# A new order of chunks and post-work in the up-projection, with the reads back of the transposed blocks issued by ScalarE

## The reference

```python
def conv_ffn(h, w_up, conv_w, conv_b, w_down):
    u = causal_dwconv(h @ w_up, conv_w, conv_b)      # D_FF = 5632, width-3 depthwise conv over tokens
    gate, val = jnp.split(u, 2, axis=-1)
    return (jax.nn.gelu(gate) * val) @ w_down

x = x + conv_ffn(rmsnorm(x, norm_ffn[l]), ffn_w_up[l], ffn_conv_w[l], ffn_conv_b[l], ffn_w_down[l])
```

## Time and profile before

| | |
|---|---|
| median of 3 runs | 2179.55 us (2175.43 to 2180.16) |
| the profiled execution | 2177.84 us |
| its span in the profile | 2176.1 us |
| PE busy | 2167.0 us |
| DVE busy | 1706.7 us |
| ACT busy | 1360.0 us |
| granted TensorE clock | 1.0 over the whole span |

### The profile page before, as it was taken

The page is one execution under the profiler, slowest core; times in us unless marked ns, Lnnn a source line. Parts: engine busy times, 40 slices in busy tenths (PEclk is TensorE's granted clock), DMA queues, the critical chain, the costliest instruction groups (busy, mean ns, idle before and its releaser), DMA issues.

```text
span 2176.1 us, 28498 instructions
## 1 busy us (share of the span) xinstructions
PE 2167.0 (100%) x9780; PEld 1795.9 (83%) x9780; DVE 1706.7 (78%) x1968; ACT 1360.0 (63%) x1950; POOL 16.6 (1%) x48
## 2 busy tenths in 40 slices
PE   9999999999999999999999999999999999999999
PEld 8888888887888888888888888888888888888887
DVE  7877866788888887887776676577888888878875
ACT  6654445677777777655555555556777777766553
POOL 2000000000000000000000000000000000000000
PEclk9999999999999999999999999999999999999999
DMA  8666667777777787666676777567877787777774
GB/s 276 218 210 211 200 191 242 218 236 239 246 248 239 245 253 237 208 223 213 228 245 201 233 263 242 186 220 217 257 229 253 229 255 232 257 237 217 238 246 156
DMA packets 269357, 500.15 MB, mean 230 GB/s; under 512 B 18928, under 2 KB 56832, under 8 KB 269136
## 3 DMA queue, kind: packets, MB, share of 16 engines
q1 hardware_dynamic: 267408, 492.78, 71.3%
q0 software_dynamic: 1424, 5.60, 0.7%
q10 hardware_dynamic: 432, 0.56, 0.1%
HBM read 457.15 MB, written 41.71 MB: 229 GB/s over the span
## 4 chain that ended last, share of the span: by engine, by line
PE 82%; DVE 7%; DMA 4%; ACT 3%; issue 3%; SPq 0%; ACTq 0%; DVEq 0%
PE ps L1186 16%; PE ps L1188 16%; PE ps L1187 16%; PE ps L1081 7%; PE ps L1083 7%; PE ps L1082 7%; PE ps L1058 4%; DMA h<-turn_line 2%; PE ps L1092 2%; PE ps L1094 2%; PE ps L1093 2%; DVE w_lo L1419 2%; PE ps L1062 2%; ACT w_hi L620 1%; DMA raw<-w_down 1%
## 5 line engine op out<-in xcount | busy, mean ns | idle before, releaser
L1419 DVE TENSOR_TENSOR w_lo<-raw,w_hi 128x1024 fp32r<-128x1024 f32 x744 | 897.9, 1222 | 347.2 <-ACT w_hi L620 334.6
L620 ACT ACTIVATE w_hi<-raw 128x1024 fp32r<-128x1024 f32 x744 | 770.9, 1053 | 441.4 <-PE ps L1188 165.2
L1186 PE MATMUL ps<-w_hi,xs 128*128 128x512 f32 x1904 | 743.2, 390 | 0.3 <-DVE w_lo L1419 0.3
L1187 PE MATMUL ps<-w_lo,xs 128*128 128x512 f32 x1904 | 740.8, 389 | 0.0
L1188 PE MATMUL ps<-w_hi,xs 128*128 128x512 f32 x1904 | 740.8, 389 | 0.0
L1186 PEld LDWEIGHTS ps<-w_hi,xs 128*128 128x128 f32 x1904 | 357.4, 188 | 75.7 <-DVE w_lo L1419 2.1
L1188 PEld LDWEIGHTS ps<-w_hi,xs 128*128 128x128 f32 x1904 | 357.4, 188 | 74.6
L1187 PEld LDWEIGHTS ps<-w_lo,xs 128*128 128x128 f32 x1904 | 357.5, 188 | 73.5
L1081 PE MATMUL ps<-w_hi,act 128*128 128x512 f32 x736 | 286.9, 390 | 0.4 <-DVE w_lo L1419 0.2
L1082 PE MATMUL ps<-w_lo,act 128*128 128x512 f32 x736 | 286.4, 389 | 0.0
L1083 PE MATMUL ps<-w_hi,act 128*128 128x512 f32 x736 | 286.4, 389 | 0.0
(11 more groups left out here) (312 smaller groups left out, 2004.8 us busy)
## 6 DMA issues: line engine op xcount, KB each, us to landing
raw<-w_up SPq DMA_DIRECT2D x352, 512.0 KB, 4.4
raw<-w_in SPq DMA_DIRECT2D x191, 512.0 KB, 4.5
raw<-w_down SPq DMA_DIRECT2D x176, 512.0 KB, 4.8
turn_line<-cross SPq DMA_DIRECT2D x284, 128.0 KB, 2.4
h<-turn_line SPq DMA_DIRECT2D x71, 512.0 KB, 5.3
raw<-w_out SPq DMA_DIRECT2D x64, 512.0 KB, 4.8
prob_line<-probs_t SPq DMA_DIRECT2D x12, 192.0 KB, 3.7
probs<-prob_line SPq DMA_DIRECT2D x3, 768.0 KB, 6.3
```

What stands on the lines that cost most here:

```text
L620: act_f(w_hi[:, s, :, :], raw[:, s, :, :], ACT.Copy).then_inc(hi_ready, 1)
L1186: mm(out, x_hi, w_hi[:, s, u, :], start=first and u == 0 and not (begun and t == 0), stop=False)
L1187: mm(out, x_hi, w_lo[:, s, u, :], start=False, stop=False)
L1419: tt(w_lo[:, s, :, :], raw[:, s, :, :], w_hi[:, s, :, :].bitcast(F32), ALU.subtract).then_inc(lo_ready, 1)
```

## The change

In the fast pairs the chunks come in another order: half 0's chunks 0 to 6, then chunk 0 of half 1, then the fast pair at steps 8 and 9, then half 1's chunks 1 to 6. PE waits for the turn of the previous half 1 ahead of step 7. The copy moves from step 10 to 11, the adds from steps 11, 12 and 4 to 12, 13 and 3; part 1 of the adds now waits for the fast products themselves. In the post-work, half 0 is scaled and turned at step 14 (before: 13) and half 1 at step 4 of the next pair (5). The taps of both halves come one step later than before, and so do their adds; gelu moves from stage 15 to 16, the split of `act` from stage 15 to 16 on ACT and 17 on DVE, which is one or two steps into the pair after. Puts stand behind loads 2 and 8. The read back is issued by ACT at stage 10, between its own instructions, with the same two waits; before each turn DVE gets a wait for `put_out`. The first chunk of a half starts its banks in all cases.

```diff
 UP_CHUNKS = ([(0, c) for c in range(KC)] + [(1, c) for c in range(KC)],
-             [(0, c) for c in range(KC - 2)] + [(0, UP_PAIR), (1, UP_PAIR), (0, KC - 2)] + [(1, c) for c in range(KC - 1)])
+             [(0, c) for c in range(UP_PAIR)] + [(1, 0), (0, UP_PAIR), (1, UP_PAIR)] + [(1, c) for c in range(1, UP_PAIR)])
-UP_LAST = KC
-UP_FOLD_AT = (11, 12, 4)
-UP_COPY_AT = 10
+UP_COPY_AT, UP_FOLD_AT = 11, (12, 13, 3)
+TURN_AT, TAPS_AT, ADDS_AT, GELU_AT = (6, 4), (12, 13, 14), (14, 15), 16
+SPLIT_AT = (16, 17)
+PUT_AT, FETCH_AT = (2, KC), 10
...
-        def fetch_up(ph, j, half):
...
+        def move_up(ph, j, i):
+
+            if i in PUT_AT:
+                put(ph.n_up + 2 * j + PUT_AT.index(i))
...
                 load(w_up[ph.layer], ph.q_up + 4 * j, i, bass.ds(j * NB + half * D_FF, NB), p)
-                if i % KC == 1:
-                    put(ph.n_up + 2 * (j - 1) + i // KC)
-                if i % KC == 3:
-                    fetch_up(ph, j - 1, i // KC)
+                move_up(ph, j - 1, i)
...
                 if i < KC:
                     mlp_post(KC + c, ph, 0, j - 1, fast_last)
                     mlp_post(c, ph, 1, j - 1, fast_last)
+                    if not (isinstance(j, int) and j == 1):
+                        mlp_post(2 * KC + c, ph, 1, j - 2, None)
                 else:
+                    mlp_post(2 * KC + c, ph, 0, j - 1, None)
                     mlp_post(KC + c, ph, 1, j - 1, fast_last)
                     mlp_post(c, ph, 0, j, fast)
...
-            if stage == 5:
+            if stage == TURN_AT[half]:
...
-            if stage == 11:
+            if stage == FETCH_AT:
+
+                if not (isinstance(k, int) and k == 0):
+                    eng.wait_ge(conv_done, k)
+                eng.wait_ge(put_out, 16 * QUADS * (ph.m_up + 2 * j + half + 1))
+                eng.dma_start(h_quads[:, :, :], turn_line[:, :, :]).then_inc(moved, 16)
+            if stage == TAPS_AT[0]:
                 eng.wait_ge(moved, 16 * (ph.m_up + 2 * j + half + 1))
...
-            if stage == 15 and half == 0:
+            if stage == GELU_AT and half == 0:
                 eng.wait_ge(conv_done, k + 1)
...
-            if stage == 15 and half == 1:
+            if stage == SPLIT_AT[0] and half == 1:
...
-                if i == (UP_FAST_AT if fast else KC):
+                if i == UP_CHUNKS[fast].index((1, 0)):
                     pe.wait_ge(acc_drained, ph.n_up + 2 * j)
...
             if part == 1:
-                eng.wait_ge(chunk_used, chunk_end(q, UP_LAST))
+                eng.wait_ge(up_used, f + 1)
...
                 eng.wait_ge(rows_scaled, ph.scaled_up + 2 * j + half + 1)
+                eng.wait_ge(put_out, 16 * QUADS * (ph.m_up + 2 * j + half))
                 step(v.transpose(flip_by_seq[:, 0], flip_from[:, 4 * half]))
```

More of the change, by code:

```diff
@@ L549, in _ @@
                 load(w_down[l], ph.q_down, i, slice((2 * j + half) * NB, (2 * j + half + 1) * NB), p)
[L550 to L553, removed]
+                move_up(ph, PAIRS - 1, i)
                 if l and i - 4 in FLIPS:
@@ L774, in mlp_post @@
                     act_f(by_quad(pad[:, t, 0:S]), h_tiles[:, :, t, :], ACT.Identity, scale=w, bias=b)
-            if stage == 12:
+            if stage == TAPS_AT[1]:
                 for t in range(BT):
@@ L779, in mlp_post @@
                 ins.then_inc(tap_first, 1)
-            if stage == 13:
+            if stage == TAPS_AT[2]:
                 for t in range(BT):
@@ L1027, in _ @@
                 if i < FC:
+                    if i < KC:
+                        mlp_post(2 * KC + i, ph, 1, PAIRS - 2, None)
                     mlp_post(KC + i, ph, 0, PAIRS - 1, False)
@@ L1150, in up_products @@
             product(UP_ONE, x(0, 0), w(c, 0), True, True)
-            product(0, x(0, 1), w(c, 1), False, False).then_inc(chunk_used, 1)
+            product(0, x(0, 1), w(c, 1), False, True).then_inc(chunk_used, 1)
             pe.wait_ge(lo_ready, RING * q + c + 2)
-            product(4, x_sum(2), w(c + 1, 1), True, False).then_inc(chunk_used, 1)
+            product(4, x_sum(2), w(c + 1, 1), False, False).then_inc(chunk_used, 1)
             pe.wait_ge(up_split, 2 * f + 1)
@@ L1158, in up_products @@
             product(UP_SIX, x_sum(0), diff(2), True, True)
-            product(1, x(1, 1), diff(3), False, False).then_inc(up_used, 1)
+            product(1, x(1, 1), diff(3), False, True).then_inc(up_used, 1)
         def up_pair(ph, j, fast):
@@ L1172, in up_pair, with chunk_values @@
                 elif p != UP_PAIR:
-                    chunk_values(q, i, 4 * half, i in (0, UP_LAST + 1), i in (UP_LAST, 2 * KC - 1), p, half == 1)
-        def chunk_values(q, c, bank, first, last, p=None, begun=False):
+                    chunk_values(q, i, 4 * half, p == 0, i == 2 * KC - 1, p)
+        def chunk_values(q, c, bank, first, last, p=None):
             s, turn = c % RING, q + c // RING
@@ L1185, in chunk_values @@
                     out = ps[:, bank + t, :]
-                    mm(out, x_hi, w_hi[:, s, u, :], start=first and u == 0 and not (begun and t == 0), stop=False)
+                    mm(out, x_hi, w_hi[:, s, u, :], start=first and u == 0, stop=False)
                     mm(out, x_hi, w_lo[:, s, u, :], start=False, stop=False)
@@ L1820, in up_pair @@
                     mlp_post(c, ph, 1, j - 1)
+                    if not (isinstance(j, int) and j == 1):
+                        mlp_post(2 * KC + c, ph, 1, j - 2)
                 else:
+                    mlp_post(2 * KC + c, ph, 0, j - 1)
                     mlp_post(KC + c, ph, 1, j - 1)
@@ L1833, in mlp_post @@
                 eng.wait_ge(acc_drained, n + 1)
-            if stage == 13:
+            if stage == ADDS_AT[0]:
                 eng.wait_ge(tap_first, k + 1)
@@ L1838, in mlp_post @@
                 step(tt(to, to, tap_t[:, :, :], ALU.add))
-            if stage == 14:
+            if stage == ADDS_AT[1]:
                 eng.wait_ge(tap_last, k + 1)
@@ L1845, in mlp_post @@
                 eng.wait_ge(conv_done, k + 1)
-            if half and stage >= 14:
+            if half and stage >= ADDS_AT[1]:
                 g = ph.layer * PAIRS + j
-                if stage == 14:
+                if stage == ADDS_AT[1]:
                     eng.wait_ge(gelu_done, g + 1)
@@ L1851, in mlp_post @@
                     eng.wait_ge(prod_ready, g + 1)
-                if stage == 15:
+                if stage == SPLIT_AT[1]:
                     eng.wait_ge(act_hi, g + 1)
@@ L2242, in _ @@
                 if i < FC:
+                    if i < KC:
+                        mlp_post(2 * KC + i, ph, 1, PAIRS - 2)
                     mlp_post(KC + i, ph, 0, PAIRS - 1)
```

## The result

The changed kernel takes 2199.97 us (median of 4 runs, 2197.49 to 2201.59) against 2179.44 for the kernel before: a ratio of 1.0093, interval 1.0078 to 1.0108, 20.5 us slower. The forecast was 2197, in a range of 2184 to 2218.

What follows compares the result with a forecast made beforehand. PE bounds the kernel, issuing a matmul every 0.2267 us and losing only 5.6 us to waits. Stall A 14.0 plus stall B 9.6 less old stalls 5.6 gives +18.0 us: 2197 us forecast, range 2184 to 2218.

Steps and rivals of the forecast that it cites:

- No matmul saved, at most 5.6 us to win: Pair loop of up: the same 189 matmuls a pair, so only PE's present waits, some 5.6 us, can be won.
- Stall A: PE at step 16 waits for w_lo(16): 0.78 us behind each of the 18 fast pairs, 14.0 us in all.
- the run: DVE's work behind the fast pair, 10.99 us without idle time, from w_lo(13) to w_lo(16), starting at T+4.72.
- T: The moment PE starts the chunk that follows the fast pair; the forecast's times in a pair count from it.
- the old stalls: PE's waits in the kernel before, mostly for up_lo ahead of the fast pair's products: 5.6 us, forecast to go.
- Stall B: PE before the next fast pair waits for w_lo(24), set by half 0's read back: 0.6 us, 16 pairs, 9.6 us.
- my walk: Step-by-step timing behind the fast pair; half 0's read goes out at T+18.5 and lands at T+23.5, releasing the taps.
- I am wrong if ... ACT's taps never wait for h: Sign against the forecast, which had ACT wait for h before pad_g's taps by 1 us or more.
- What a second queue does to the first: Read on ACT's ring beside SP's loads: by the skill's rule it gets no faster, B at or above its value.
- Load 25 hidden by 1 us: Load 25, behind half 1's put, lands at T+34.2; the differences that need it come at T+35.2.
- Moving reads off SP worth nothing: Earlier loads gain nothing more, as ACT waited for w_up loads only 3.1 us in layer 0's up.

Runs made afterwards that it cites:

- The best kernel found: both16 with the writes of half 1 put behind load 25, not load 24: 2172.41 us, ratio 0.9966 to the kernel before.
- The order alone: The changed kernel with the reads back on SP, behind loads 20 and 26, the rest as it is: 2194.68 us, ratio 1.0068.
- both16: The changed kernel with half 1's last tap's add and product behind w_lo(16), splits of act one step later: 2181.19 us, ratio 1.0010.
- both16_put9: both16 with the writes of half 1 put behind load 25, not load 24: 2172.41 us, ratio 0.9966.
- prod16: The changed kernel with only half 1's product moved behind w_lo(16), splits of act one step later: 2193.38 us, ratio 1.0064.

## Why the prediction was right, point by point

**No matmul saved, at most 5.6 us to win.** Held as far as the runs can tell. The best kernel found wins 6.6 us, 5.0 to 9.8 by its interval.

**Stall A, 0.78 us, 14.0 us in all.** The mechanism held: the run starts at 632.91, T+4.69 (forecast T+4.72), goes through to the end of the product at 643.78, and w_lo(16) lands too late for step 16. Moving two instructions out of the run takes A away. The size was too small. The term that was mis-sized is the last gap of the run: I took the run of the earlier trace rows whole, with some 0.1 us between product and w_lo, but at step 16 a new turn of the hardware loop begins, and w_lo(16) starts 0.53 us after the product ends (0.52 to 0.56 at all 14 turns). A came to 1.16 us. Where the same step lies outside the loop the gap is less, and so is PE's wait. VectorE at the loop's exit in layer 0:

```profile
...
821.05 1.23 DVE L1858 TENSOR_TENSOR pad_v<-pad_v,pad_g 128x1024 f32<-128x1024 f32 x1
822.49 1.23 DVE L1423 TENSOR_TENSOR w_lo<-raw,w_hi 128x1024 fp32r<-128x1024 f32 x1 [0.21 <-DVE pad_v L1858]
...
```

The 15.9 us of idle time at L1190 hide part of it, since the record of the last matmul runs 0.16 us past the time at which the next was due. With that and the 0.11 of the second matmul A is 15.9 + 18 x 0.27 = 20.8 us. The order alone fits this: 20.8 less the 5.6 of the old stalls is 15.2, against 15.7 measured there.

**Stall B, 0.6 us, 9.6 us in all.** The size held, by luck: 4.8 us of idle time in 11 waits, with 0.27 each some 7.8 us, and the taps of step 20 start at T+23.7 (median) against the T+23.5 of my walk. The mechanism failed, and by a sign that I had set myself: "I am wrong if ... ACT's taps never wait for h". They never do. The step that failed is what ends the wait ahead of them. I had ScalarE issue the read at T+18.5, land 5.0 us later and keep the taps waiting. It issued it at T+16.2, before w_hi(17) had begun, and it landed at T+20.4 (medians; 4.1 us for the reads of both halves below), 3.2 us ahead of the taps. The taps were late because w_hi(20) was, and that because load 20 goes out only after w_lo(16), late by A's run, at T+17.6 where I had +17, and then, beside the read, takes 5.1 us (medians) where I had 4.4. I had w_hi(20) done at T+22.5 in passing, one microsecond off the gate, and did not see that it was as near to deciding as the read; it was done at T+23.7. So a read that I had landing 3.1 us too late and a w_hi(20) that I had done 1.2 us too early left the taps near their place:

```profile
...
raw<-w_up SPq DMA_DIRECT2D x152, 512.0 KB, 4.5
...
h<-turn_line ACTq DMA_DIRECT2D x20, 512.0 KB, 4.1
...
```

**The old stalls, 5.6 us, go.** Held: no wait for up_lo is left. The sum is 20.8 + 7.8 - 5.6 = 23.0 us, against 23.7 between the spans and 20.5 between the medians.

**What a second queue does to the first.** A read issued 0.6 us ahead on ScalarE's queue holds up the load on SP's: w_hi(19) followed the issue of its load after 5.84 us, and after 4.22 where the read stood behind it. That is the longest case; the medians of the landings are 4.6 and 4.0 us. The Trainium skill (DMA: Bandwidth & Descriptors, Issuing engines are not separate DMA queues) says that such transfers interleave on the same 16 DMA engines. The runs agree with it as far as a load beside such a read lands later. I had applied it to the read only, and what it costs is the load.

**Load 25 hidden by 1 us.** Held in the changed kernel (L1771 waits for raw in one pair of 16, by 0.5 us), and it became the limit as soon as A was gone, as both16 and both16_put9 show.

**Moving reads off SP worth nothing.** Wrong for the kernel before (14 us slower), and a loss of about 5 us in the new order, but close to right in the new order with every w_lo in time (1.6 us).

## What to carry to other kernels

When an order is shifted against a ring of prefetched chunks, count for each result how many chunks ahead of its user it lands, before and after; work that moved by one step while the consumer moved by two has lost a whole chunk. The order in which one engine issues its transfers can look like a restriction and be a priority: a read moved to another engine's program went out ahead of the load that was wanted first. Two stalls in one loop can be one chain: removing one without the other (prod16) gave most of the time to the other. And when a forecast of the time comes out, look at the waits that it rests on before believing its mechanism.

## What was not expected of the hardware

ScalarE's DMA issue at 644.46 falls while the ACTIVATE of 643.93 still runs and 0.43 us before the next (L613, at 644.89) starts, although two ACTIVATEs, w_hi(17) and w_hi(18), stand between that one and the read in the code. So an issue does not wait for the instructions ahead of it to run. It does stand behind one that waits, as the read at 629.67 behind the copy at 629.59 shows.

A turn of the hardware loop costs VectorE time in one place and nothing in another. The trace has the branch, between the product and w_lo(16), 14 times taken and twice at the loop's exit:

```profile
...
L2237 DVEq COMPARE_BRANCH  x16: 50/56/69, 510.7 to 1916.7; - x16
...
```

In the changed kernel VectorE's program waits, just ahead of the branch, until its own product is done. The gap is 0.52 to 0.56 us at each of the 14 turns and 0.21 at the two exits. In both16 the branch stands behind w_lo(15) with no such wait, and w_lo(16) follows with no gap:

```profile
...
591.78 2.36 DVE L1423 TENSOR_TENSOR w_lo<-raw,w_hi 128x1024 fp32r<-128x1024 f32 x2
...
```

So the turn is hidden behind the instruction that is running, unless a wait for that same instruction stands ahead of it. Part of what both16 gains over the changed kernel is this gap, 0.4 us a pair as an estimate: 0.53 less the 0.12 that lie between product and w_lo in both16, where no turn stands between them (596.63 to 596.75).
